# The first four loads of x on ScalarE's queue, the first weights alone on SyncE's

## The reference

```python
def rmsnorm(x, g):
    xf = x.astype(jnp.float32)
    y = xf * lax.rsqrt(jnp.mean(xf * xf, axis=-1, keepdims=True) + EPS)
    return (y * g.astype(jnp.float32)).astype(x.dtype)

def hybrid_ab(h, w_in, conv_w, conv_b, ga_w, ga_b, gx_w, gx_b, lam, w_out):
    proj = h @ w_in
    y, xr, q, k, v, g = jnp.split(proj, [L, 2 * L, 2 * L + R, 2 * L + 2 * R, 2 * L + 3 * R], axis=-1)
    ...
```

## Time and profile before

| | |
|---|---|
| median of 3 runs | 1387.8 us |
| lowest, highest | 1382.7, 1388.54 us |
| span of the profiled execution (first to last instruction) | 1382.0 us |
| instructions | 22584 |
| TensorE busy | 1365.3 us (99%) |
| VectorE, ScalarE, GpSimd busy | 846.8 (61%), 661.8 (48%), 147.4 us (11%) |
| DMA: moved, mean rate | 215.29 MB, 156 GB/s |

### The profile page before, as it was taken

One profiled execution on the slowest core, in us unless ns is written; L12 is line 12 of the kernel. 1 busy time (PEld: TensorE's weight loads), 2 busy tenths in 40 slices (PEclk: granted clock), 3 DMA queues, 4 the chain that ended last, 5 costly groups with the idle time before them and its releaser, 6 DMA issues.

```text
span 1382.0 us, 22584 instructions
## 1 busy us (share of the span) xinstructions
PE 1365.3 (99%) x9250; PEld 1170.3 (85%) x9250; DVE 846.8 (61%) x1299; ACT 661.8 (48%) x1170; POOL 147.4 (11%) x131
## 2 busy tenths in 40 slices
PE   8999999999999999999999999999999999999999
PEld 8988888889955888888887877888888888879999
DVE  6976887656867678885734467433333456775554
ACT  6646555544366465555433446332233346555442
POOL 0010111001310001110004000111011100301110
PEclk9999999999999999999999999999999999999999
DMA  8535667556497455555433210232222234414553
GB/s 306 192 122 183 214 218 251 196 187 200 161 345 263 163 183 192 188 187 182 153 103 103 84 62 32 76 105 94 92 92 92 92 113 140 155 58 153 192 184 123
DMA packets 60967, 215.29 MB, mean 156 GB/s; under 512 B 6721, under 2 KB 12737, under 8 KB 57409
## 3 DMA queue, kind: packets, MB, share of 16 engines
q1 hardware_dynamic: 56272, 206.59, 44.7%
q10 hardware_dynamic: 4592, 7.26, 1.4%
HBM read 208.59 MB, written 1.05 MB: 152 GB/s over the span
## 4 chain that ended last, share of the span: by engine, by line
PE 91%; DVE 4%; ACT 2%; DMA 1%; issue 1%; POOL 0%; SPq 0%; DVEq 0%; ACTq 0%; POOLq 0%
PE psum L330 18%; PE psum L320 16%; PE psum L321 16%; PE psum L322 16%; PE psum L329 8%; PE psum L1275 3%; PE psum L1300 2%; PE psum L317 2%; PE psum L318 2%; PE psum L319 2%; PE psum L1438 2%; DVE WL L252 1%; PE psum L2740 1%; DMA stage<-ab_in 1%; PE psum L1631 1%; PE psum L332 1%
## 5 line engine op out<-in xcount | busy, mean ns | idle before, releaser
L252 DVE TENSOR_TENSOR WL<-stage,WH 128x1024 fp32r<-128x1024 f32 x332 | 419.0, 1303 | 236.0 <-ACT WH L247 235.8
L247 ACT ACTIVATE WH<-stage 128x1024 fp32r<-128x1024 f32 x332 | 333.0, 1051 | 206.7 <-PE psum L322 150.3
L320 PE MATMUL psum<-XX,WH 128*128 128x256 f32 (+1 forms) x1208 | 391.5, 324 | 6.1 <-DVE WL L756 1.7
L321 PE MATMUL psum<-XX,WH 128*128 128x256 f32 (+1 forms) x1208 | 384.5, 318 | 0.0
L322 PE MATMUL psum<-XX,WL 128*128 128x256 f32 (+1 forms) x1208 | 384.2, 318 | 0.0
L330 PE MATMUL psum<-XX,WH 128*128 128x512 f32 x832 | 288.2, 397 | 0.0
L320 PEld LDWEIGHTS psum<-XX,WH 128*128 128x128 f32 x1208 | 229.0, 190 | 36.5 <-issue 9.4
L322 PEld LDWEIGHTS psum<-XX,WL 128*128 128x128 f32 x1208 | 229.1, 190 | 16.1
L321 PEld LDWEIGHTS psum<-XX,WH 128*128 128x128 f32 x1208 | 229.2, 190 | 16.1 <-issue 0.5
L329 PE MATMUL psum<-XX,WL 128*128 128x256 f32 x728 | 203.2, 279 | 0.9 <-DVE WL L252 0.9
L330 PEld LDWEIGHTS psum<-XX,WH 128*128 128x128 f32 x832 | 150.1, 188 | 29.5 <-issue 1.2
(11 more groups left out here) (298 smaller groups left out, 1900.6 us busy)
## 6 DMA issues: line engine op xcount, KB each, us to landing
stage<-w SPq DMA_DIRECT2D x132, 512.0 KB, 4.6
stage<-merge SPq DMA_DIRECT2D x80, 512.0 KB, 4.6
ring<-ada SPq DMA_DIRECT2D x24, 1024.0 KB, 6.0
stage<-in SPq DMA_DIRECT2D x44, 512.0 KB, 4.6
stage<-ab_in SPq DMA_DIRECT2D x22, 512.0 KB, 5.9
stage<-nsa_in SPq DMA_DIRECT2D x20, 512.0 KB, 4.8
stage<-out SPq DMA_DIRECT2D x16, 512.0 KB, 4.8
stage<-ab_out SPq DMA_DIRECT2D x8, 512.0 KB, 4.4
```

What stands on the lines that cost most here:

```text
L247: e.activation(hi, raw, ACT.Copy).then_inc(s_hi, 1)
L252: e.tensor_tensor(lo, raw, hi.bitcast(F32), ALU.subtract).then_inc(s_lo, 1)
L320: e.matmul(dst, wh, xh, start=start, stop=False)
L321: e.matmul(dst, wh, xl, start=False, stop=False)
```

## The change

```diff
@@ hybrid_scalar
         def hybrid_scalar(e, flow):
+            xT = A["xT"].rearrange("p (k n) -> p k n", k=8)
             e.dma_start(par[:, :], A["params"]).then_inc(s_const[1], 16)
+            for j in range(4):
+                e.dma_start(X[:, 2 * j:2 * j + 2, NOW], xT[:, 2 * j:2 * j + 2, :]).then_inc(s_x[j], 16)
 
             e.wait_ge(*ve.of("h.warm"))
@@ hybrid_sync
         def hybrid_sync(e, flow, rings):
-            xT = A["xT"].rearrange("p (k n) -> p k n", k=8)
             ms = list(flow.ahead())
             for j in range(4):
-                e.dma_start(X[:, 2 * j:2 * j + 2, NOW], xT[:, 2 * j:2 * j + 2, :]).then_inc(s_x[j], 16)
                 src, raw, _, _ = quarter(j)
                 e.dma_start(raw, src).then_inc(s_quarter[j], 16)
```

## The result

The changed kernel takes 1389.65 us (median of 20 runs, 1386.04 to 1392.67). The kernel before takes 1386.09 us (20 runs, 1382.7 to 1389.15). The ratio is 1.0027, with a 95% interval of 1.0019 to 1.0036: slower by 3.6 us, which is real and within 0.5%. The profiled execution of after has a span of 1388.0 us and a mean granted clock of 0.996.

A forecast was written before the change was run, and what follows sets the result against it. PE, busy 1365.3 of 1382.0 us, bounds the kernel; the start hangs on landing order. Chunk 1 moves 1.2 us, chunk 3 between 0.9 and 1.9, middle +1.4: 1387.8 + 1.4 = 1389.2 us, range 1383.0 to 1392.4.

The forecast's parts named there:

- order of issue between transfers: DMA at the start: transfers land in order of issue, sharing with the one beside; x3 1.9 us later, at 12.4.
- rival of strict alternation: DMA at the start: every packet of x pays for a packet of weights; chunk 1 +3.3 us, 1390.7 total; chance 0.25.
- the 0.8 us for a busy ScalarE: Upper bound before chunk 1: x2 lands close before x3, so ScalarE's 1.6 us per quarter adds up to 0.8.
- The middle case: Start: x3 at 12.4, chunk 1 at 16.2, +1.4 us in total, 1389.2 us; chance 0.47.
- the DMA engines are full from 2 us on: DMA at the start: earlier issue of the weights is worth nothing by itself; share 0.93 from 2 to 6 us.
- the late starts of the two constants: ScalarE's queue before: small constants landed 7.2 us after issue, large ones moved behind 17; taken as evidence against alternation.
- The first product: PE's start: x0 lands behind 0.9 MB, so the first product comes 2.9 us later, at about 9.7.
- the four issues on ScalarE: ScalarE's start: table load and Exp move back 1.96 us, Exp ends at 4.7, covered by waiting for x0; at most 0.05 us.
- The 1 KB pieces of x: DMA at the start: under alternation x yields two to four bytes to the larger weight packets for each of its own.
- Chunk 3's wait of 0.37 us: PE before chunk 3: the wait absorbs part of chunk 1's 1.2 us, so PE's side moves by 0.9 us.
- The fall of the clock at the start: PE's first products: a long stand lowers the clock, 1.4 to 7.1 us; 1398.0 with alternation; slower by over 0.5%, chance 0.04.
- outlasts most of chunk 1: PE in chunks 0 and 1: only a low clock lasting that long decides for slower by over 0.5%; 48 products cost 5.7 us.

The follow-up runs named there:

- exchanged roles: Against the changed kernel, SyncE issues the four transfers of x, then m2 and m3, and ScalarE issues params and the four quarters; 1386.84 us, 1.0004 of before.

## Why the prediction was right, and which step in it was wrong

**Time, sign and size class** were right: 1389.2 forecast, 1389.65 measured, within 0.5%. But two errors met in it, and that it came within 0.5 us is luck. The shift was forecast at +1.4 us and is +3.6 (+3.0 on equal clock), and the median of before was 1387.8 from 3 runs and is 1386.1 from 20. The scatter of before (1382.7 to 1388.5) was, to judge by the later series, in the main the second fall, which the prediction took as scatter and didn't explain.

**The step that failed** is "I take order of issue between transfers, and sharing with the one beside it". What happened is nearest to the rival of strict alternation: weights up to m3 passed x3, and the packets counted 198 against 198 and 179 against 179. Between these stretches, with 543 of x to 316, the alternation was not strict. The rival's sum fits better than its terms: x3 was to land 3.2 us later, at 13.7, and landed at 14.5, but the 0.8 us for a busy ScalarE did not come on top; from x3's high part to chunk 1 it was 3.85 us, forecast 3.83; chunk 1 was to start at 18.3, and started at 18.45; the time was to be 2.9 us up, and is 3.0 to 3.6. The middle case had x3 at 12.4, chunk 1 at 16.2 (1.2 us later, where 3.5 were measured) and chunk 3 at 29.6 to 30.6. That the DMA engines are full from 2 us on was wrong too: both queues together moved 198 GB/s from 2 to 6 us, less than the 228 of before. The evidence that I set against alternation, the late starts of the two constants, was of another kind: a transfer issued behind a long backlog started some 3 us late on its queue, for a reason that no run here showed, but in the first five microseconds there is no backlog and both queues start together. Two tests told it: with the quarters split (1 KB against 1 KB, issued at half the rate) the loss was gone, and with m2 and m3 held back x3 came 2.4 us earlier, though the time did not follow until the clock was mended too.

**The first product** was forecast at 9.7 and came at 10.09: here the middle case and the rival lie too close together to be told apart by it.

**What the steps got right.** No cost of the four issues on ScalarE shows: exchanged roles, with four issues there too, give 1.0004. The table load and the Exp ended at 5.31 (forecast 4.7; the four issues took 2.6 us and not 1.96), covered by the wait for x0, which ended at 7.88. ScalarE doesn't wait for m2. The 1 KB pieces of x were named as the reason. Chunk 3's wait of 0.37 us went, and the load of the gates had time enough: its product follows without a wait.

**What went beyond it.** The fall of the clock at the start, priced at 1.4 to 7 us in the rival, did come, and lasted 3.4 to 6.8 us, through 14 to 26 products. But it cost the changed kernel little (marks 378.96 and 379.29 without it, 379.07 to 380.60 with it), since slow products fill the time in which x is missing. Where x comes earlier, with m2 and m3 held back, it costs 1.85 us. The rival's condition "outlasts most of chunk 1" was not met: it ended within chunk 0, in the slowest profile with its third quarter, at 18.2. In 12 to 14 us the DMA's share was 0.60 at 204 GB/s, with little left of x and of the issued weights, and later weights waiting for low parts.

**What the notes say.** By the Trainium skill, "DMA: Bandwidth & Descriptors", section "Queues, rings and completion order", each engine goes round its queues packet by packet, where a packet is a group of typically 9 to 17 descriptors that is finished before the turn passes on. A packet of the profile is one contiguous piece, so equal counts of pieces are not what the section states. A transfer of x is 272 of the profile's packets, 17 for each engine, and a quarter or a half 144, 9 for each: turns by such groups would give 17 to 9, and 543 to 316 in 5 to 9 us lies near it, while 198 to 198 and 179 to 179 do not. The trace does not say which engine moved a packet, so how turns are taken stays open. By the Trainium skill, same page, section "Issuing engines are not separate DMA queues", only issue time is saved. No run gained time by it; split quarters and exchanged roles show no change (1.0002, 1.0004), and the changed kernel lost 3 us, which the section does not lead one to expect.

## What to carry to other kernels

Of two queues that were busy together here, the one with the larger contiguous pieces got the larger part in bytes (0.35 MB to 0.18, 0.65 to 0.53, 0.62 to 0.17). So put a critical load with small pieces ahead of the large ones on one queue, or make the pieces alike, before spreading it over queues. Where two things bound a start, mend both before calling either harmless. Compare kernels at a mark ahead of the places where the clock may fall, and sort runs by their mean clock, before a few microseconds are put down to an edit. A stand of 2 to 3 us for a DMA in a stretch with little TensorE work was followed by a spell at half clock in all seven profiles that had one, worth 1.5 to 5 us; 1.89 us of idle products in its place cost 0.2 us or less in their profile.

## What the runs showed of the hardware that was not expected

- Two busy queues moved equal numbers of packets in some stretches, 198 to 198 in 2 us with pieces of 1 and 2 KB, 179 to 179 with 1, 2 and 4 KB in the mix, and 543 to 316 in the 4 us between.
- Stands of 2.6 to 4.1 us before the first product, behind 7 warm-up products, ended at 1.2 GHz (a granted clock of 0.50) for 3.4 to 6.8 us; behind 15 warm-ups there was no such spell.
- In the modulation, in a stretch where PE stood on and off for other reasons too, the seven profiles with a wait of 2.1 to 3.4 us had a spell at the lower level behind it, and five of the six with 0.5 to 1.3 us had none. A mean clock of 0.998 or less shows such spells in 27 of 35 executions of before on one chip and 21 of 35 on another.
- Before its first change, the record of the clock reads 1.00 while products are at half pace (22 in 4 us).
